# All 31 taps of a depthwise convolution moved to TensorE as plain fp32 column tiles over four shifted copies

## The reference, cut to what matters

```
def conformer_conv(va, vg, p):
    u = va * jax.nn.sigmoid(vg)
    u = depthwise_conv(u, p["conv_w"], p["conv_b"], CONV_PAD)      # 31 taps, padding 15 and 15
    return jax.nn.silu(layernorm(u, p["ln_g"], p["ln_b"]))
...
    va, vg, ga, xb, gb = jnp.split(z, ...)                          # z = h @ w_in, 512 x 5120
    y_a = conformer_conv(va, vg, p) * jax.nn.silu(ga)
    y_b, hT = rglru_branch(xb, p, h0, True)                         # 4-tap conv, gates, two linear scans
    y_b = y_b * jax.nn.silu(gb)
    return jnp.concatenate([y_a, y_b], axis=-1) @ p["w_out"], hT
```

## Time and profile before

| what | value |
|---|---|
| median of three runs | 1827.26 us (1826.8 to 1828.82) |
| the profiled execution's own time | 1828.44 us |
| its span, first to last instruction | 1827.1 us |
| TensorE (PE) busy | 1749.3 us, 96% |
| VectorE (DVE) busy | 1059.6 us, 58% |
| ScalarE (ACT) busy | 758.7 us, 42% |
| granted TensorE clock, mean | 0.976 of full |

### The profile page before, as it was taken

The page is one execution under the profiler, slowest core; times in us unless marked ns, Lnnn a source line. Parts: engine busy times, 40 slices in busy tenths (PEclk is TensorE's granted clock), DMA queues, the critical chain, the costliest instruction groups (busy, mean ns, idle before and its releaser), DMA issues.

```text
span 1827.1 us, 19870 instructions
## 1 busy us (share of the span) xinstructions
PE 1749.3 (96%) x8054; PEld 1411.2 (77%) x8054; DVE 1059.6 (58%) x1450; ACT 758.7 (42%) x1028; POOL 18.9 (1%) x39
## 2 busy tenths in 40 slices
PE   6899999999999999999889998999989999999996
PEld 4688888888778788888677865776778788888885
DVE  4766799899775756663455353444546644444333
ACT  3587654654442433333333544433433332322221
POOL 0000000000000000000000000000000000000000
PEclk9999999999898999999999998999999999999998
DMA  7344433333323232223222121222122222323321
GB/s 313 118 169 141 159 116 125 129 116 127 120 90 102 81 103 93 92 93 104 91 70 84 55 69 46 67 72 69 65 75 92 92 93 93 102 95 103 101 96 46
DMA packets 49963, 185.81 MB, mean 102 GB/s; under 512 B 5392, under 2 KB 5392, under 8 KB 49616
## 3 DMA queue, kind: packets, MB, share of 16 engines
q1 hardware_dynamic: 42624, 155.21, 25.2%
q0 software_dynamic: 4848, 17.80, 3.0%
q10 hardware_dynamic: 2400, 11.53, 1.6%
HBM read 182.42 MB, written 2.10 MB: 101 GB/s over the span
## 4 chain that ended last, share of the span: by engine, by line
PE 84%; DVE 7%; ACT 6%; issue 2%; ACTq 1%; DMA 0%; DVEq 0%
PE banks L1439 25%; PE banks L1441 24%; PE banks L1440 24%; PE banks L1471 2%; PE banks L1703 2%; ACT w_hi L389 1%; PE banks L1459 1%; PE banks L1452 1%; PE banks L1725 1%; PE banks L1747 1%; PE banks L1793 1%; DVE w_lo L816 1%; DVE u L950 1%; ACTq L415 1%; DVE h_lo L889 1%
## 5 line engine op out<-in xcount | busy, mean ns | idle before, releaser
L1439 PE MATMUL banks<-h_hi,w_hi 128*128 128x512 f32 x1408 | 559.3, 397 | 10.5 <-DVE h_lo L825 5.0
L1441 PE MATMUL banks<-h_hi,w_lo 128*128 128x512 f32 x1408 | 551.8, 392 | 0.0
L1440 PE MATMUL banks<-h_lo,w_hi 128*128 128x512 f32 x1408 | 551.4, 392 | 0.0
L816 DVE TENSOR_TENSOR w_lo<-raw,w_hi 128x1024 fp32r<-128x1024 f32 x292 | 355.4, 1223 | 290.1 <-ACT w_hi L389 289.8
L389 ACT ACTIVATE w_hi<-raw 128x1024 fp32r<-128x1024 f32 x292 | 304.2, 1051 | 153.9 <-PE banks L1441 142.5
L1439 PEld LDWEIGHTS banks<-h_hi,w_hi 128*128 128x128 f32 x1408 | 265.9, 189 | 79.1 <-issue 13.5
L1441 PEld LDWEIGHTS banks<-h_hi,w_lo 128*128 128x128 f32 x1408 | 266.2, 189 | 56.8
L1440 PEld LDWEIGHTS banks<-h_lo,w_hi 128*128 128x128 f32 x1408 | 266.5, 189 | 53.9 <-issue 0.7
L1011 DVE SCALAR_TENSOR_TENSOR U<-U,vec 128x512 f32<-128x512 f32 x112 | 83.3, 744 | 0.0
L1439 PE MATMUL banks<-y_hi,w_hi 128*128 128x512 f32 x192 | 76.9, 400 | 5.6 <-ACT gs L689 5.5
L1441 PE MATMUL banks<-y_hi,w_lo 128*128 128x512 f32 x192 | 75.7, 394 | 0.0
(11 more groups left out here) (349 smaller groups left out, 2283.9 us busy)
## 6 DMA issues: line engine op xcount, KB each, us to landing
raw<-weights SPq DMA_DIRECT2D x292, 512.0 KB, 3.2
mraw<-modw POOLq DMA_DIRECT2D x32, 512.0 KB, 4.0
mod<-modw ACTq DMA_DIRECT2D x4, 2048.0 KB, 23.1
X<-x_in ACTq DMA_DIRECT2D x1, 2048.0 KB, 13.5
out<-X SPq DMA_DIRECT2D x4, 512.0 KB, 2.7
ctx_x<-ctx_in ACTq DMA_DIRECT2D x1, 1024.0 KB, 19.8
cst<-consts POOLq DMA_DIRECT2D x1, 448.0 KB, 3.6
vec<-vecs POOLq DMA_DIRECT2D x1, 291.0 KB, 6.5
```

The source lines that it names most:

```text
L816: tt(slot(w_lo, c), slot(raw, c), slot(w_hi, c).bitcast(F32), ALU.subtract).then_inc(S["lo"], 1)
L1439: mm(o, wh, r_hi, start=start, stop=False)
L1440: mm(o, wh, r_lo, start=False, stop=False)
L1441: return mm(o, wl, r_hi, start=False, stop=stop)
```

## The change

All 31 taps go to TensorE, and both `dg` chunks, the taps on VectorE and the split of the input tile go away. Four copies of a 32-channel group, shifted by 0, 8, 16 and 24 tokens, are put under one another on the 128 partitions (`rep`, for each pass four groups side by side, two buffers), by 16 DMAs from SBUF to SBUF for each pass, issued by SyncE's queue ahead of the new chunk `cw`. A matmul with a 128x32 stationary block then does four taps of 32 channels at once, and eight steps by four groups make 32 matmuls of plain fp32, each group into its own 32 partitions of bank 3. The chunk `cw` is used as loaded, without a split (`WHOLE`), and the slot behind it in the ring is freed by the matmuls and not by VectorE's split. ScalarE takes the result from PSUM with the bias, VectorE adds it to the sum. The weights of a step lie at the taps' places, and the 32nd tap is zero.

```
-PE_TAPS = 16
+RW = T + 8
...
-        s += [("xb", i), ("gb", i), ("ga", i), ("gx", i), ("dg", i, 0), ("dg", i, 1)]
+        s += [("xb", i), ("gb", i), ("ga", i), ("gx", i), ("cw", i)]
...
+        def replicas(i):
+            e.wait_ge(S["uu"], i + 1)
+            if i > 1:
+                e.wait_ge(S["mm"], C["cw", i - 2] + 1)
+            for j in range(4):
+                for s in range(4):
+                    n = T + 7 if s < 3 else T + 6
+                    e.dma_start(rep[i % 2][32 * s:32 * s + 32, j * RW:j * RW + n],
+                                U[32 * j:32 * j + 32, (i + 1) * UW + 8 * s:(i + 1) * UW + 8 * s + n]).then_inc(s_rep[i % 2], 16)
...
         for c in range(N_CHUNKS):
+            if WHOLE[c]:
+                replicas(NAMES[c][1])
             if c >= RING:
-                e.wait_ge(S["lo"], c - RING + 1)
+                if WHOLE[c - RING]:
+                    e.wait_ge(S["mm"], c - RING + 1)
+                else:
+                    e.wait_ge(S["lo"], N_SPLIT[c - RING] + 1)
             e.dma_start(slot(raw, c), wts[c, :, :]).then_inc(s_raw[c % RING], 16)
...
+        def convolved(i):
+            product("cw", i)
+            fn(tile(U, i, T, UW), bank(3), ACT.Identity, bias=cb2[:, i:i + 1]).then_inc(S["cpe"], 1)
...
-            fn(us_hi[:, :], tile(U, i + 1, UW), ACT.Copy).then_inc(S["ushi"], 1)
...
+        def convolved(i):
+            e.wait_ge(S["cpe"], i + 1)
+            if i:
+                e.wait_ge(S["csum"], i)
+            tt(csum[:, :], csum[:, :], tile(U, i, T, UW), ALU.add).then_inc(S["csum"], 1)
...
-            low(us_lo[:, :], tile(U, i + 1, UW), us_hi[:, :]).then_inc(S["uslo"], 1)
-            head_input(NT + i, T, tap)
+            head_input(NT + i, T)
...
-            tt(acc, bank(3), acc, ALU.add).then_inc(S["cpe"], 1)
...
-            for half in range(2):
-                c = ready("dg", i, half)
...
-                for b in range(KC):
-                    k = 8 * half + b
-                    last = three(bank(3), c, b, us_hi[:, k:k + T], us_lo[:, k:k + T], k == 0, k == PE_TAPS - 1)
-                last.then_inc(S["mm"], 1)
+            c = C["cw", i]
+            e.wait_ge(s_raw[c % RING], 16 * (c // RING + 1))
+            e.wait_ge(s_rep[i % 2], 256 * (i // 2 + 1))
+            if i:
+                e.wait_ge(S["cpe"], i)
+            for step in range(8):
+                for j in range(4):
+                    a = j * RW + step
+                    last = mm(banks[32 * j:32 * j + 32, 3 * 512:4 * 512], slot(raw, c, (8 * j + step) * 32, 32), rep[i % 2][:, a:a + T],
+                              start=step == 0, stop=step == 7)
+            last.then_inc(S["mm"], 1)
...
-    nc = bacc.Bacc("TRN2", target_bir_lowering=False, num_devices=1)
+    nc = bacc.Bacc("TRN2", target_bir_lowering=False, num_devices=1, dynamic_dma_scratch_size=4096)
```

More of the change, by code:

```diff
@@ L90 @@
 N_CHUNKS = len(NAMES)
+WHOLE = [n[0] == "cw" for n in NAMES]
+N_SPLIT = [sum(not q for q in WHOLE[:c]) for c in range(N_CHUNKS)]
 def bank_uses():
@@ L122 @@
     "norm_t norm_hi norm_lo xp conv uhi ulo gread e2 mv sq thr scan sig uu "
-    "ushi uslo tgt sgb sgat sga cpe csum yact ybhi yblo mod_v ymu usum usq yln ysil yga yhi yalo res xsq xsum "
+    "tgt sgb sgat sga cpe csum yact ybhi yblo mod_v ymu usum usq yln ysil yga yhi yalo res xsq xsum "
     "lpad lcp dhi dsub dlo gsil gy gyhi gylo ores osq osum hsum "
@@ L210, in program @@
     s_mod0 = [ctx.enter_context(nc.semaphore(f"s_mod0_{j}")) for j in range(4)]
+    s_rep = [ctx.enter_context(nc.semaphore(f"s_rep{s}")) for s in range(2)]
     s_mraw = [ctx.enter_context(nc.semaphore(f"s_mraw{s}")) for s in range(MOD_RING)]
@@ L237, in program @@
     mraw = p("mraw", MOD_RING * CW)
-    us_hi = p("us_hi", UW, F32R)
-    us_lo = p("us_lo", UW, F32R)
+    rep = [p(f"rep{k}", 4 * RW) for k in range(2)]
     csum = p("csum", T)
@@ L383, in hi @@
         def hi(c):
-            if c >= N_CHUNKS:
+            if c >= N_CHUNKS or WHOLE[c]:
                 return
@@ L501, in act @@
             head_roots(i, TC)
-        e.wait_ge(S["uu"], NT)
+        def convolved(i):
+            product("cw", i)
+            fn(tile(U, i, T, UW), bank(3), ACT.Identity, bias=cb2[:, i:i + 1]).then_inc(S["cpe"], 1)
         for i in range(NT):
             ahead("xb", i)
-            if i:
-                product("dg", i - 1, 1)
-            fn(us_hi[:, :], tile(U, i + 1, UW), ACT.Copy).then_inc(S["ushi"], 1)
             product("xb", i)
             head_input(NT + i, T, 0)
+            if i:
+                convolved(i - 1)
             ahead("gb", i)
@@ L521, in act @@
             head_gates(NT + i, T, [bank(b) for b in range(4, 8)])
-            ahead("dg", i, 0)
-            ahead("dg", i, 1)
+            ahead("cw", i)
             head_roots(NT + i, T)
@@ L526, in act @@
             fn(tile(yb_hi, i), u[:, :], ACT.Copy).then_inc(S["ybhi"], 1)
+        convolved(NT - 1)
         for k in range(NT + 1):
@@ L812, in lo @@
         def lo(c):
-            if c >= N_CHUNKS:
+            if c >= N_CHUNKS or WHOLE[c]:
                 return
-            e.wait_ge(S["hi"], c + 1)
+            e.wait_ge(S["hi"], N_SPLIT[c] + 1)
             tt(slot(w_lo, c), slot(raw, c), slot(w_hi, c).bitcast(F32), ALU.subtract).then_inc(S["lo"], 1)
@@ L935, in dve, with head_input @@
         own.did(e.memset(csum[:, :], 0.0))
+        for k in range(2):
+            own.did(e.memset(rep[k][96:128, :].rearrange("p (j w) -> p j w", w=RW)[:, :, T + 6:T + 7], 0.0))
         e.memset(xp[:, :], 0.0).then_inc(S["pad"], 1)
-        def head_input(I, w, between):
+        def head_input(I, w):
             def sw(k):
@@ L945, in head_input, with head_drive @@
             own.did(ts(u[:, 0:w], xp[:, 0:w], sw(0), col("sconv_b", I % NT), ALU.mult, ALU.add))
-            n = own.n
             for k in range(1, SCONV_K):
-                between()
-                own.wait(n)
+                own.wait()
                 m = stt(u[:, 0:w], xp[:, k:k + w], sw(k), u[:, 0:w], ALU.mult, ALU.add)
                 if k < SCONV_K - 1:
-                    n = own.did(m)
+                    own.did(m)
             m.then_inc(S["conv"], 1)
-            between()
             e.wait_ge(S["uhi"], I + 1)
             low(u_lo[:, 0:w], u[:, 0:w], u_hi[:, 0:w]).then_inc(S["ulo"], 1)
-        def head_drive(I, w, between):
+        def head_drive(I, w):
             for k in range(2):
@@ L961, in head_drive, with head_scan @@
                 stt(th[k][:, 0:w], tr[k][:, 0:w], 1.0, th[k][:, 0:w], ALU.add, ALU.mult).then_inc(S["mv"], 1)
-                between()
                 own.did(stt(ti[k][:, 0:w], ti[k][:, 0:w], 1.0, u[:, 0:w], ALU.add, ALU.mult))
-                between()
-        def head_scan(I, w, init, between):
+        def head_scan(I, w, init):
             for k in range(2):
@@ L981, in head_scan @@
                                          ALU.mult, ALU.add).then_inc(S["scan"], 1)
-                between()
         for i in range(NT):
             ahead("xc", i)
-            head_input(i, TC, lambda: None)
+            head_input(i, TC)
             ahead("vg", i)
@@ L992, in dve @@
             ahead("gc", i)
-            head_drive(i, TC, lambda: None)
-            head_scan(i, TC, lambda k: 0.0, lambda: None)
+            head_drive(i, TC)
+            head_scan(i, TC, lambda k: 0.0)
             e.wait_ge(S["scan"], i + 1)
@@ L997, in dve @@
                 own.did(e.tensor_copy(ctx_state[:, 2 * i + k:2 * i + k + 1], tr[k][:, (TC - 1, 0)[k]:(TC, 1)[k]]))
-        for i in range(NT):
[L1000 to L1012, removed]
+        def convolved(i):
[3 more added lines that the diff above has]
+            tt(csum[:, :], csum[:, :], tile(U, i, T, UW), ALU.add).then_inc(S["csum"], 1)
+        for i in range(NT):
             ahead("xb", i)
-            e.wait_ge(S["ushi"], i + 1)
-            low(us_lo[:, :], tile(U, i + 1, UW), us_hi[:, :]).then_inc(S["uslo"], 1)
-            head_input(NT + i, T, tap)
+            head_input(NT + i, T)
+            if i:
+                convolved(i - 1)
             ahead("gb", i)
-            tap()
             e.wait_ge(S["tgt"], i + 1)
             stt(tg[:, :], tg[:, :], 1.0, bank(1), ALU.add, ALU.mult).then_inc(S["sgb"], 1)
-            tap()
             ahead("ga", i)
@@ L1026, in dve @@
             stt(tile(sga, i), tile(sga, i), 1.0, bank(0), ALU.add, ALU.mult).then_inc(S["sga"], 1)
[L1027 to L1032, removed]
+            head_drive(NT + i, T)
+            ahead("cw", i)
+            head_scan(NT + i, T, lambda k: ctx_state[:, 2 * i + k:2 * i + k + 1])
             e.wait_ge(S["scan"], NT + i + 1)
-            n = own.did(tt(u[:, :], tr[0][:, :], tr[1][:, :], ALU.add))
-            own.wait(tap_n[0])
-            product("dg", i, 1)
-            tt(acc, bank(3), acc, ALU.add).then_inc(S["cpe"], 1)
+            own.did(tt(u[:, :], tr[0][:, :], tr[1][:, :], ALU.add))
             e.wait_ge(S["sgb"], i + 1)
-            own.wait(n)
```

(11 more changed lines are left out.)

## The result

The changed kernel takes 1796.73 us (median of four runs, 1793.85 to 1799.05), the kernel before 1828.04 beside it: 31.3 us less, ratio 0.9827 with a 95% interval of 0.9807 to 0.9847. I had forecast 1855 us, slower, with a chance of 0.63 for slower. It is faster, and it stands where the first rival put it, 1796 us.

A forecast was written before the change was run, and what follows sets the result against it. TensorE was taken to bound the mixer loop. The convolution's +3.3 us a pass, +26.2 for eight, on 1828.44 gave 1854.6, stated as 1855 us, other terms 0; the range was 1794 to 1885 us.

The forecast's parts named there:

- the first rival: Convolution on TensorE: four column tiles stream side by side, 7.1 us a pass, 32 us off, 1796 us; chance 0.33.
- Part 2: TensorE's convolution: program order lets only two records overlap, 14.4 us for 11.13, +3.3 us a pass, +26.2 for eight.
- What bounds the kernel: Mixer loop: TensorE, busy all 34.00 us of a pass, sets the pace, with VectorE close behind at 31.05.
- Part 1: VectorE and ScalarE relief in the loop: credited nothing; the chain between gx products shortens by 12 us to some 18.
- The lower bound: Convolution of a pass with four tiles fully side by side: 16 records each of 0.43 us, no faster than 6.9 us.
- The switch: TensorE entering and leaving the column tiles around the convolution: 0.1 us to enter, as much to leave by estimate.
- Part 3: Weight loads of the convolution: hidden under the 0.43 us of the record ahead, counted as 0.
- Part 4: SyncE's queue and the copies: 17 DMAs a pass at about 0.49 us an issue, covered by 10 us, counted as 0.
- Part 5: The mixer loop's ends: last csum and shortened chain end well before the final sum of tiles; no change.
- The second: Rival for the convolution: records run one after another, 27.7 us, +16.6 for each pass, 1961 us; chance 0.10.
- The third: Rival: pairs with weight loads in the open, 32 slots of 0.54 to 0.57 us, 1883 to 1890 us; chance 0.09.
- The fourth: Rival: copies late on SyncE's queue if small DMAs were issued every 2 us, about 100 us in all; chance 0.03.

The follow-up runs named there:

- no_taps: The kernel before the change with 14 of VectorE's 15 taps left out: 1827.06 us beside 1828.85, ratio 0.9992.
- one_tile: The changed kernel with 29 of the 32 convolution matmuls of a pass writing into column tile 0: 1942.37 us.
- tile_major: The changed kernel with the matmuls reordered, all eight steps of one column tile before the next tile's: 1921.08 us.
- copies_twice: The changed kernel with the copies left out in passes 2 to 7: 1797.55 us, ratio 0.9829 to the kernel before.
- copies32: The changed kernel with each of the 16 copies of a pass cut into two of half the width: 1811.04 us.
- the edit: The changed kernel with mod chunks 24 and 25 moved ahead of the last convolution: 1792.71 us; later 1791.9 beside 1797.1 for the changed kernel on one chip.

## Why the prediction was wrong

The step that failed is in Part 2: records start in order, so two of them stream side by side and never four, 33 slots and 14.4 us for the convolution. The runs show four side by side, 16 slots and 7.01 us. Over eight passes the step is worth 8 x 7.4 = 59 us, and the forecast missed by 58.

**What bounds the kernel** was right. TensorE had no gap before and has none after, and its stream per pass is the time: 8 x 3.93 us are all of the gain.

**Part 1** was right that VectorE's relief is worth nothing by itself (`no_taps`), less so in a size. The chain from the gates to u_lo is 22.3 us in the changed kernel (341.55 to 363.85), not some 18: it lost 7.4 us, not 12, since VectorE now stands for ScalarE for 7.3 us of it. It has 4.7 us left ahead of gx at 368.6; in a kernel with less cover the error would have shown in the time.

**Part 2 failed, at the step from the rows' order to two records side by side.** The step said: the second record of tile 0 waits 0.43 us for the first, and tile 1's first record stands behind it. The first half is true. The second half took "waits for its tile" for "holds the queue". The runs show that up to three records wait for a tile without holding up the next: 16 slots instead of 33. (If the unit is the matmul, a second matmul waits for a tile in the same way; the slots are the same.) The rows that I had the earlier trace rows are of one tile only, where a strict order and a waiting place for each tile look the same; they could not choose between them. With 6.9 and 27.5 us as bounds, and a rule of order that no row tested, nothing earned the forecast its 0.42 against 0.33 for the first rival. The lower bound itself was right: 6.9 us, 7.01 measured. The switch costs some 0.3 us in all, 0.1 inside the convolution and 0.2 at its two ends, where I had 0.2.

The Trainium skill ("TensorE: Matmul & The Clock Gate", Part 3: Packing small matmuls) gave both: that distinct column tiles run concurrently, with which the trace agrees (starts of four tiles within 0.02 us, and 16 slots against the 58 of `one_tile`), and that matmuls start strictly in program order. If the records are issued as the loop has them, the second does not hold between tiles, and the measurement decides: by strict order `tile_major` would take 61 slots, and it took 52, because tile 1 starts while three earlier records of tile 0 wait.

**Part 3** was right: four loads take 0.13 us inside a slot of 0.43.

**Part 4** was right in the result (`copies_twice`, 0) and off in a size: an issue took 0.68 us, not 0.49, so the copies hold the queue for 10.84 us instead of 8, and are there 9 us before they are needed instead of 10.

**Part 5** was right: the stretch behind the loop is the same, and it is where the next 5 us lay.

**The rivals.** The first, 1796 us, is what happened, by its mechanism and its number (1796.73). The second (1961) is what `one_tile` looks like, 1942. The third has nothing for it: no load stands in the open. (Its sum is off as well: 32 slots of 0.54 to 0.57 us and 0.2 are 17.5 to 18.4 us, not 18 to 18.7, so that the upper end of the range would be some 4 us lower.) The fourth did not happen; `copies32` shows what it would look like, at twice the issues.

## What to carry to other kernels

Plain fp32 matmuls in 32-column tiles cost here as much as the fullest column tile: share the work out evenly among the tiles, and go round them in short turns. Four records (two plain fp32 matmuls) in a row cost nothing, eight doubled the time of the convolution; what lies between was not run. When a forecast hangs on a queueing rule, ask whether the rows could tell it from its rival at all; if they could not, weigh the bounds and not the rule. With TensorE as the bound, taking work from a busy VectorE bought nothing here, and the copies made by DMA were free as long as their issues, some 0.65 us each, fitted ahead of the next load in the queue.

## What was not expected of the hardware

- One streaming and three waiting records for each column tile fit all the orders: 7.01 and 7.08 us (two and four records in a row), 15.80 (eight), 22.54 (sixteen). One matmul of two records that streams and one that waits fits them too. Where the waiting places lie, and whether weight loads count in them, stays open; row tiles and other types were not tried.
- Plain fp32 into four column tiles, at full clock, starts four records every 0.43 us, the time that one record takes with a tile alone: 0.11 us for each record of 512 columns.
- Halving the copies hardly made an issue cheaper (0.63 against 0.68 us).
- The granted clock fell to 1.2 GHz behind 3.6 us of two-column matmuls without a pause, and cost the convolution there 1.7 us (both runs with the edit; the cause was not tested apart).
